# Windowed attention: the mask summed into the scores by TensorE, exponentials read from PSUM, the scaled residual made one stage earlier

## The reference, cut to what matters

```python
def sliding_window_attention(q, k, v, sinks):      # blocks of 128 tokens, 8 query heads, 2 key heads
    kb, vb = band(k), band(v)                      # the previous block and the own one: 256 keys
    scores = einsum('bnqgrd,bnkgd->bngrqk', q, kb) * (HEAD_DIM ** -0.5)
    scores = where(valid, scores, NEG_INF)         # a causal window of 128 keys
    probs = softmax(concatenate([scores, sink]))[..., :-1]
    return einsum('bngrqk,bnkgd->bnqgrd', probs, vb)

proj = x @ w_in + b_in                             # q, k, v, u, g
attn = sliding_window_attention(q, k, v, sinks)
sgu = u * (causal w_spatial @ layer_norm(gelu(g)) + b_spatial)
mix = concatenate([attn, sgu]) @ w_out + b_out
h = layer_norm(DEEPNORM_ALPHA * x + mix)
```

## Time and profile before

| what | value |
| --- | --- |
| median of 3 runs | 3271.71 us (3263.75 to 3277.16) |
| the profiled execution | 3279.78 us; span 3277.0 us |
| mean granted TensorE clock | 0.975 of full speed |
| busy, whole span | PE 95%, DVE 82%, ACT 55%, POOL 24% |
| attention stage, first to last instruction | 1903.94 to 1958.14 us |

### The profile page before, as it was taken

How to read it: one execution, slowest core, us unless ns; L and a number is a source line. 1 busy time by engine, 2 the same in 40 slices (tenths; PEclk the granted TensorE clock), 3 DMA queues, 4 the chain that set the end, 5 groups by cost and what they waited for, 6 DMA issues and landing times. The chain is left out here.

```text
span 3277.0 us, 47202 instructions
## 1 busy us (share of the span) xinstructions
PE 3109.3 (95%) x16174; PEld 2689.7 (82%) x16174; DVE 2679.8 (82%) x3857; ACT 1815.7 (55%) x2204; POOL 780.9 (24%) x497
## 2 busy tenths in 40 slices
PE   7998799998999999999999877999999999999998
PEld 6996678998998888888888756788888888888885
DVE  6997635993976888787788565999999999999997
ACT  4453533343873333333333442787787778778775
POOL 0000103454003444444444000221112112111212
PEclk9999799999999999999999889999999999999999
DMA  4230033334567999899998213999999999999996
GB/s 131 78 88 29 1 128 113 122 133 154 229 249 298 331 361 348 317 331 340 343 340 300 82 57 142 346 358 364 364 360 363 363 364 363 368 371 366 369 370 249
DMA packets 194742, 850.53 MB, mean 260 GB/s; under 512 B 21793, under 2 KB 103329, under 8 KB 151057
## 3 DMA queue, kind: packets, MB, share of 16 engines
q1 hardware_dynamic: 166704, 698.17, 58.3%
q0 software_dynamic: 27936, 151.02, 11.3%
HBM read 808.49 MB, written 58.46 MB: 265 GB/s over the span
## 5 line engine op out<-in xcount | busy, mean ns | idle before, releaser
L3344 DVE TENSOR_TENSOR moe_w_lo<-all_raw,moe_w_hi 128x2048 fp32r<-128x2048 f32 x298 | 676.1, 2287 | 50.4 <-ACT moe_w_hi L3270 48.1
L3270 ACT ACTIVATE moe_w_hi<-all_raw 128x2048 fp32r<-128x2048 f32 x298 | 569.3, 1916 | 80.0 <-PE moe_GU L3209 59.1
L3209 PE MATMUL moe_GU<-moe_w_hi,moe_x_lo 128*128 128x512 f32 x1056 | 412.2, 390 | 0.0
L3208 PE MATMUL moe_GU<-moe_w_lo,moe_x_hi 128*128 128x512 f32 x1056 | 412.1, 390 | 0.0
L3207 PE MATMUL moe_GU<-moe_w_hi,moe_x_hi 128*128 128x512 f32 x1056 | 411.7, 390 | 0.0
L2026 DVE SCALAR_TENSOR_TENSOR experts_pair<-experts_pair,all_x_first 128x1024 f32<-128x1024 f32 x128 | 156.4, 1222 | 147.8 <-DMA experts_pair<-in_peer_pairs,experts_slot 147.8
L1860 POOL COPY experts_slot<-all_pair_id 128x1 uint32 x128 | 152.7, 1193 | 489.1 <-DVE all_h L2038 310.5
L1863 POOL DMA_INDIRECT experts_pair<-in_peer_pairs,experts_slot x128 | 222.0, 1734 | 114.7 <-POOL experts_slot L1860 110.1
L3208 PEld LDWEIGHTS moe_GU<-moe_w_lo,moe_x_hi 128*128 128x128 f32 x1056 | 198.6, 188 | 42.1
L3209 PEld LDWEIGHTS moe_GU<-moe_w_hi,moe_x_lo 128*128 128x128 f32 x1056 | 198.6, 188 | 41.6
L3207 PEld LDWEIGHTS moe_GU<-moe_w_hi,moe_x_hi 128*128 128x128 f32 x1056 | 198.9, 188 | 40.6
(11 more groups left out here) (579 smaller groups left out, 8234.4 us busy)
## 6 DMA issues: line engine op xcount, KB each, us to landing
all_raw<-in_w_moe SPq DMA_DIRECT2D x149, 2048.0 KB, 9.7
all_hT<-in_w_moe SPq DMA_DIRECT2D x49, 2048.0 KB, 9.6
all_wu<-in_peer_pairs SPq DMA_DIRECT2D x64, 1024.0 KB, 9.9
all_hT<-in_peer_wdT SPq DMA_DIRECT2D x122, 512.0 KB, 11.9
peer_gates<-gates_out SPq DMA_DIRECT2D x6, 4096.0 KB, 12.1
experts_gt<-peer_gates SPq DMA_DIRECT2D x32, 768.0 KB, 9.9
all_hT<-in_w_in SPq DMA_DIRECT2D x40, 512.0 KB, 3.9
all_hid<-peer_early SPq DMA_DIRECT2D x60, 192.0 KB, 7.4
```

The lines of the kernel that those rows point to most:

```text
L3208: pe.matmul(out, x_hi[:, kx, :], lo[:, k, :], start=False, stop=False)
L3209: mm = pe.matmul(out, x_lo[:, kx, :], hi[:, k, :], start=False, stop=(kx == KD - 1))
L3270: act.activation(w_hi[p % RING][:], piece_of(r, p), ACT.Copy).then_inc(w_high, 1)
L3344: dve.tensor_tensor(w_lo[p % RING][:], piece_of(r, p), w_hi[p % RING][:].bitcast(F32), ALU.subtract).then_inc(w_low, 1)
```

## The change

The mask is now converted to fp32r and summed into the scores by a second product of the identity matrix with the mask, one for each of the four products of a unit. The maxima are taken from PSUM, with the factor 1/8 applied to the four maxima; the exponentials read PSUM and apply the 1/8 themselves. The score buffer is therefore free after `exps`, not after the first pass of `maxes`. The first pass on VectorE is gone. The four passes `h * ALPHA + out_bias` and the load of `out_bias` go to the projection stage.

```diff
 stage_project2, SyncE
                     if n >= 2 + RAWS:
                         sp.wait_ge(w_low, n - RAWS + 1)
+                        sp.dma_start(c.out_bias, a["b_out_2"].to_broadcast([P, D])).then_inc(bb_in, 16)
                     sp.dma_start(w[:, n % RAWS, :, :], ...
 stage_project2, VectorE, at the end
+                dve.wait_ge(bb_in, 16)
+                dve.wait_ge(turned, 2 * M)
+                for m in range(M):
+                    h = c.h[:, m, :]
+                    dve.scalar_tensor_tensor(out=h, in0=h, scalar=ALPHA, in1=c.out_bias,
+                                             op0=ALU.mult, op1=ALU.add).then_inc(pre_ok, 1)
 stage_attention, SyncE
-                sp.dma_start(c.out_bias, a["b_out_2"].to_broadcast([P, D])).then_inc(bb_in, 16)
 TensorE, scores(i)
                     if i >= 2:
-                        pe.wait_ge(s_read, i - 1)
+                        pe.wait_ge(exped, i - 1)
                     for r in range(4):
-                        mm = pe.matmul(S[:, i % 2, r, lo:lo + width], ..., start=True, stop=True)
+                        out = S[:, i % 2, r, lo:lo + width]
+                        pe.matmul(out, ..., start=True, stop=False)
+                        if i == 0 and r == 0:
+                            pe.wait_ge(mask_ok, 2)
+                        mm = pe.matmul(out, ident_r[:], mask_r[:, lo:lo + width], start=False, stop=True)
 ScalarE, exps(i)
                     act.wait_ge(maxed, i + 1)
+                    if i >= DEEP:
+                        act.wait_ge(turned, 2 * (i - DEEP) + 2)
                     for r in range(4):
-                        act.activation(sc[:, b, r, lo:lo + width], sc[:, b, r, lo:lo + width], ACT.Exp,
-                                       bias=top[:, b, 0, r:r + 1], accum_out=top[:, b, 2, r:r + 1])
+                        act.activation(sc[:, b, r, lo:lo + width], S[:, i % 2, r, lo:lo + width], ACT.Exp,
+                                       scale=64 ** -0.5, bias=top[:, b, 0, r:r + 1], accum_out=top[:, b, 2, r:r + 1])
 ScalarE, ahead of exps(0)
+                act.activation(ident_r[:], c.ident[:], ACT.Copy).then_inc(mask_ok, 1)
+                act.wait_ge(masked, 3)
+                act.activation(mask_r[:], mask[:], ACT.Copy).then_inc(mask_ok, 1)
 VectorE, maxes(i)
                     dve.wait_ge(s_done, i + 1)
-                    if i >= DEEP:
-                        dve.wait_ge(turned, 2 * (i - DEEP) + 2)
-                    x = sc[:, b, :, lo:lo + width]
-                    dve.scalar_tensor_tensor(out=x, in0=S[:, i % 2, :, lo:lo + width], scalar=64 ** -0.5,
-                                             in1=mask[:, lo:lo + width].unsqueeze(1).to_broadcast([P, 4, width]),
-                                             op0=ALU.mult, op1=ALU.add).then_inc(s_read, 1)
-                    dve.wait_ge(s_read, i + 1)
-                    step(dve.tensor_reduce(top[:, b, 3, :], x, AX.X, ALU.max))
+                    step(dve.tensor_reduce(top[:, b, 3, :], S[:, i % 2, :, lo:lo + width], AX.X, ALU.max))
+                    if i == 0:
+                        dve.wait_ge(sink_in, 16)
-                    step(dve.tensor_tensor(high, high, mine, ALU.max))
+                    step(dve.scalar_tensor_tensor(out=high, in0=high, scalar=64 ** -0.5, in1=mine,
+                                                  op0=ALU.mult, op1=ALU.max))
 VectorE, ahead of the loop and in it
-                dve.wait_ge(sink_in, 16)
-                dve.wait_ge(masked, 3)
-                        h = c.h[:, i // 2, :]
-                        dve.wait_ge(bb_in, 16)
-                        dve.scalar_tensor_tensor(out=h, in0=h, scalar=ALPHA, in1=c.out_bias,
-                                                 op0=ALU.mult, op1=ALU.add).then_inc(pre_ok, 1)
```

More of the change, by code:

```diff
@@ L2130, in stage_project2 @@
         (cb_in, rb_in, x_high, x_low, w_high, w_low, v_done, g_done, c_done, taken, added, gelued, chain, root,
-         var) = (s.sem(n) for n in ("cb_in", "rb_in", "x_high", "x_low", "w_high", "w_low", "v_done", "g_done",
-                                    "c_done", "taken", "added", "gelued", "chain", "root", "var"))
+         var, bb_in, pre_ok) = (s.sem(n) for n in (
+             "cb_in", "rb_in", "x_high", "x_low", "w_high", "w_low", "v_done", "g_done", "c_done", "taken", "added",
+             "gelued", "chain", "root", "var", "bb_in", "pre_ok"))
         chans = ([(c.kT[:], 4), (vT[:], 5)] + [(c.qT[:, j, :], j) for j in range(AJ)]
@@ L2333, in stage_attention @@
         mask = s.sb("mask", [P, W2])
+        mask_r = s.sb("mask_r", [P, W2], F32R)
+        ident_r = s.sb("ident_r", [P, P], F32R)
         sink = s.sb("sink", [P, 2, AJ])
@@ L2342, in stage_attention @@
         O = s.ps("O", [P, 2, 4, P])
[L2343 to L2346, removed]
+        (masked, mask_ok, sink_in, ws_in, bs_in, s_done, maxed, exped, probs, chain, turned, pt_ok, o_done, o_taken,
+         g_done, g_taken, ws_ok) = (s.sem(n) for n in (
+             "masked", "mask_ok", "sink_in", "ws_in", "bs_in", "s_done", "maxed", "exped", "probs", "chain", "turned",
+             "pt_ok", "o_done", "o_taken", "g_done", "g_taken", "ws_ok"))
         def span(n):
@@ L2385, in scores @@
                     if i >= 2:
-                        pe.wait_ge(s_read, i - 1)
+                        pe.wait_ge(exped, i - 1)
                     for r in range(4):
                         h = slice(64 * (r // 2), 64 * (r // 2) + 64)
-                        mm = pe.matmul(S[:, i % 2, r, lo:lo + width], c.qT[h, j0 + r % 2, n * P:n * P + P],
-                                       c.kT[h, (n - 1) * P + lo:(n - 1) * P + lo + width], start=True, stop=True)
+                        out = S[:, i % 2, r, lo:lo + width]
+                        pe.matmul(out, c.qT[h, j0 + r % 2, n * P:n * P + P],
+                                  c.kT[h, (n - 1) * P + lo:(n - 1) * P + lo + width], start=True, stop=False)
+                        if i == 0 and r == 0:
+                            pe.wait_ge(mask_ok, 2)
+                        mm = pe.matmul(out, ident_r[:], mask_r[:, lo:lo + width], start=False, stop=True)
                     mm.then_inc(s_done, 1)
```

## The result

The changed kernel took 3279.1 us in the median of 18 runs, the kernel before 3274.35 us in 18 runs made beside it; the ratio is 1.0028, with a 95% interval of 1.0018 to 1.0039. That is 0.28% slower, 9 us by the ratio (6 to 13), as by the means of the two; the medians lie 4.8 us apart. The range ended at 3270 us.

The account below looks back on a forecast made before the run. VectorE was taken to set the pace of the attention units, TensorE to bound projection. 7.9 us saved up to exps(7) and 2.2 us behind it, 10.1 in sum, gave a median of 3261.6 us; range 3253 to 3270 us.

Parts of the forecast that it names:

- rival B: Attention stage: TensorE stays at 1.2 GHz throughout, stage 10.8 us longer, 3282.5 us; chance 0.08.
- TensorE's work: Attention stage: each second product costs 0.30 us at full clock, 0.46 at 1.2 GHz; a pair of units 9.6 or 17.1 us.
- two changes of kind: TensorE's scores: switching between fp32 and fp32r around each mask product, about 0.10 us a switch at full clock.
- rival A: Attention stage: changes of kind are hidden, a product costs 0.12 us; 14 to 16 us saved; chance 0.18.
- The clock: TensorE in attention: 17.1 us of work a pair leaves no gaps, and such stretches rose to the full clock.
- C: Attention stage: the clock falls once again as TensorE waits for exps; saving 6 us or less, 3266 to 3269 us; chance 0.16.
- The walk: Attention stage followed unit by unit: exps(0) at 1908.3, exps(2) at 1915.9, exps(7) at 1940.0, end at 1948.0; 10.1 us saved.
- The move of the residual: Four passes and their load go to the projection stage, hidden behind TensorE's work; counted at zero there.
- three residual passes lose 1.15 us each: VectorE in attention: the three residual passes that were followed by other units save 1.15 us each.
- VectorE's work: Attention stage: without first passes and residual passes, a pair of units falls from 11.6 to 7.9 us.
- The new wait: Attention stage: scores(i + 2) waits for exps(i), not the first pass of maxes(i); costs little in steady part, more at start.

Follow-up runs that it names:

- e5_one_half: The kernel before, with all four score products of a unit taken from rows 0 to 63, other half's heads left out; 3268.31 us in one run.
- e4_mask_fp32: The changed kernel with mask and identity kept in fp32, so no score product changes precision; 3294.72 us in one run.
- e1_grouped: The changed kernel with the mask summed in first by two products of 512 columns, then the four score products together; 3264.08 us, ratio to before 0.9974.
- e6_pairs: The changed kernel reordered: two score products on different halves, their two mask products, and again; 3265.72 us, ratio to before 0.9971.
- e9_group_late: The changed kernel with units 0 to 3 interleaved and units 4 to 7 grouped, mask first; 3274.60 us in one run.
- e3_move_only: The kernel before, with only the scaled residual and its load moved to the projection stage; 3268.58 us, ratio 0.9985.
- e8_group_first: The changed kernel with units 0 to 3 grouped, mask first, and units 4 to 7 interleaved; 3264.82 us in one run.
- e7_attn_only: The changed kernel with the scaled residual and its load back in the attention stage; 3284.07 us, ratio to before 1.0031.

## Why the prediction was wrong

**The sign.** The forecast was 10 us less, rival B 10.8 us more with a chance of 0.08, and 9 us more came. B had the size, but only part of the mechanism: it let TensorE stay at 1.2 GHz through the whole stage, at 17.1 us a pair of units. What the trace shows is about 24 us at 1.2 GHz in one piece at the start, three shorter pieces of 3.4 us behind it, and pairs of 13.3 us even at the full clock. Less time at the lower clock than in B and dearer products came to about B's sum; that the sums agree is chance.

**The step that failed** is the price of the second product, in "TensorE's work": 0.30 us at the full clock, with 0.40 as the upper end. It is (3.76 - 1.07) / 4 = 0.67 us, and at 1.2 GHz (6.64 - 2.01) / 4 = 1.16 us instead of 0.46. I took the 1.07 us of the four score products as theirs wherever they stand, and added the columns of the new product and two changes of kind. The 1.07 us were those of two halves of the rows at work together. A hint of it stood in rows 3: eight fp32 instructions of 256 columns over 64 rows take 1.14 us, and eight of 128 columns over all 128 rows (the transposes at 1942.97) take 1.09 us, almost the same time for half the columns. In e5_one_half, all on one half, the eight cost 1.92 / 8 = 0.24 us each, and not 0.13. I named the halves under rival A, as a reason for less cost, and not that a product over all 128 rows between them would end it.

The parts of 0.67 us, at the full clock, are an estimate from these rows. An instruction of a score product takes 0.21 us (e5_one_half), so the overlap that is lost is 4 x 0.21 = 0.85 us a unit, 0.21 us a product; the prediction had it at nothing. The mask's columns are 0.12 us, as forecast. The rest, 0.34 us, is for changes: 0.62 us to the mask product less 2 x 0.21, and 0.32 us behind it less 0.12, is 0.20 us for each change. The prediction had taken 0.10 us from rows 5, where the change is one of operation and precision and both sides use all 128 rows; e4_mask_fp32 shows about the same 0.2 us (0.62 and 0.63 us, less 2 x 0.21) with no change of precision. A unit has eight groups, each with a change behind it, where it had one. The split rests on this reckoning; that both are lost together by the interleaving is what e1_grouped and e6_pairs show.

The Trainium skill (TensorEngine Tiling (Array Packing), "Key Properties") states both halves of it: different tiles of the array run products in parallel, and a change of the tiling mode drains the array. The runs agree, if the 0.2 us of a change are such a drain. The prediction did not weigh it, and it is the rule that speaks against this change.

**The clock** is the second step. Against B stood that at 17.1 us a pair TensorE has no gaps, and that such stretches rose to the full clock. It had no gaps, and stayed at 1.2 GHz for more than 23 us, in the changed kernel and in e9_group_late; and in the changed kernel the clock fell again at 1923.8 and 1930.7 us with no gap ahead of it, which neither B nor C (a fall for want of work) had foreseen. The Trainium skill (TensorE: Matmul & The Clock Gate, Part 1) says that sustained activity releases the lower clock. Grouped products bear that out (in e1_grouped the clock was back about 10 us into the stage); the 23 us do not, unless what these records call busy is not that activity. Which property of the interleaved groups it is, the runs don't tell: the cause of the long low stretch stays open.

**The walk** failed where these prices enter: exps(2) at 17.2 us instead of 12.0, then 38.9 us to exps(7) instead of 24.1. The tail took 9.5 us, where 8.0 were forecast.

**What was right.** The move of the residual costs the projection stage nothing: the four passes took 4.62 us and ended 7.8 us ahead of the stage's end, their load was issued some 50 us ahead of them (1829.46 to 1879.83); "three residual passes lose 1.15 us each" was too small: e3_move_only saved 6.1 us, and by its mean clock some 17 us of it stood at 1.2 GHz, where it had been some 27 us. VectorE's work fell by 12.2 us, near the 7.5 + 1.4 + 4.6 = 13.5 us worked out; 0.7 us of the difference is one small operation, L2507, that took 0.90 us once. A reduction takes 1.22 us from PSUM as from SBUF, so the Trainium skill's extra 62 cycles (VectorE: DVE Perf Modes, "The TRN2 errata") are not seen here either. The new wait costs little: with it and without interleaving the stage is 40 to 41 us. The forecast of 10 us would have held for the edit made as in e1_grouped: it saves 13.4 us in the stage, 8.5 us (0.26%, from 4 to 13 us) in the whole.

## What to carry to other kernels

Before a product is put between others on TensorE, divide the group's time by its instructions. If that is less than one of them takes alone, they overlap, as these did on different halves of the rows, and an instruction over all rows between them costs that overlap and a gap on each side; put it ahead of the group, as in e1_grouped. And where work is shifted from a busy VectorE to a TensorE that idles, price it at both clocks: a unit's interleaved scores cost 3.76 us at the one and 6.64 us at the other.

## What was not expected of the hardware

- An fp32 product over 64 rows and 256 columns costs 0.27 us among its like on both halves of the rows, 0.48 us among its like on one half (1.92 / 4), and 0.62 us alone between products over 128 rows.
- A change between instructions over 64 and over 128 rows cost about 0.2 us at the full clock, with or without a change of precision.
- TensorE was busy for 23 us without a gap at a granted clock of 0.50 (1.2 GHz), and in e8_group_first, with the first units grouped, for 23 us at 1.00; and the clock fell five times (twice in the changed kernel, twice in e7_attn_only, once in e8_group_first) with no idle time ahead of the fall.
- An exponential of 256 elements took 476 ns from PSUM and 496 ns from SBUF in the mean of 24, but the read of its sum behind it 206 ns instead of 186: together the same.
